# Queries of four tiles in one pass beside tile 0's experts, key pieces beside tile 0's choice

## What is computed

```python
h = rmsnorm(x, norm1_g)
z = h @ w_in            # qa 1024, ka 1024, va 1024, qb 512, kb 512, vb 512, forget 8, gates 2048 columns
oa = diff_attn(qa, ka, va)          # 8 heads, 2 maps each, chunk-causal, relative bias
ob = fox_attn(qb, kb, vb, cumsum(log_sigmoid(forget + b_f)))     # 8 heads, causal
x = x + (sigmoid(g_A) * (rmsnorm(oa) @ w_pa) + sigmoid(g_B) * (ob @ w_pb)) @ w_o
xb = rmsnorm(x, norm2_g)
q = xb @ peer_wq; the best 16 of 128 x 128 experts for each of 8 heads (top_k of sums of two lists)
x = x + sum over the 128 chosen experts e of  softmax_weight_e * gelu(u_e . xb) * v_e
y = rmsnorm(x, final_g)
```

## Time and profile before

| | |
|---|---|
| median of three runs | 2085.18 us |
| the profiled execution's own time | 2091.16 us |
| its span, first to last instruction | 2089.4 us |
| PE, PEld busy | 1615.2, 1017.9 us (77%, 49%) |
| DVE busy | 1505.3 us (72%) |
| ScalarE, POOL busy | 540.9, 748.5 us (26%, 36%) |
| mean granted TensorE clock | 0.903 |
| moved by DMA | 753.80 MB, mean 361 GB/s |

### The profile page before, as it was taken

How to read it: one execution, slowest core, us unless ns; L and a number is a source line. 1 busy time by engine, 2 the same in 40 slices (tenths; PEclk the granted TensorE clock), 3 DMA queues, 4 the chain that set the end, 5 groups by cost and what they waited for, 6 DMA issues and landing times.

```text
span 2089.4 us, 22180 instructions
## 1 busy us (share of the span) xinstructions
PE 1615.2 (77%) x7119; PEld 1017.9 (49%) x7119; DVE 1505.3 (72%) x3453; ACT 540.9 (26%) x1429; POOL 748.5 (36%) x697
## 2 busy tenths in 40 slices
PE   7988899798877877989778767868886755666655
PEld 5778785375445724764466323535673222222211
DVE  1011219688887686889876999878688899988886
ACT  3242212111731221247402325732022210100111
POOL 0000000555443333234423444334255544555552
PEclk9998999999998988999889989988998878888888
DMA  7832774999999999999999989998999999999996
GB/s 229 303 116 77 270 242 139 393 421 419 424 420 421 421 376 400 381 396 358 361 398 420 409 348 396 361 399 337 421 404 421 397 398 421 396 422 421 422 408 265
DMA packets 129396, 753.80 MB, mean 361 GB/s; under 512 B 16992, under 2 KB 33296, under 8 KB 42880
## 3 DMA queue, kind: packets, MB, share of 16 engines
q0 software_dynamic: 78336, 570.46, 67.1%
q1 hardware_dynamic: 28432, 155.19, 19.9%
q10 hardware_dynamic: 22512, 26.73, 3.7%
HBM read 732.32 MB, written 19.48 MB: 360 GB/s over the span
## 4 chain that ended last, share of the span: by engine, by line
PE 36%; DMA 25%; DVE 24%; issue 8%; ACT 5%; ACTq 1%; POOL 1%; another core or an unknown queue 0%; SPq 0%; DVEq 0%; POOLq 0%; PEldq 0%
DMA ring<-in_uv,stage 19%; PE pz L1341 9%; DVE ring L2096 8%; PE acc L1681 7%; PE pz L1330 7%; DVE vsum L2123 5%; DMA wbuf<-in_w_q 2%; PE ps L1639 2%; PE ps L1602 1%; PE ps L1582 1%; DMA wbuf<-in_w_o 1%; DVE diag L2107 1%; DMA wbuf<-in_w_pa 1%; DMA zt<-F 1%; PE po L1424 1%
## 5 line engine op out<-in xcount | busy, mean ns | idle before, releaser
L876 POOL DMA_INDIRECT ring<-in_uv,stage x544 | 689.4, 1267 | 946.3 <-DVE vsum L2123 356.1
L1681 PE MATMUL acc<-ring,diag 128*128 128x512 f32 (+1 forms) x1068 | 599.5, 708 | 266.2 <-DVE diag L2107 208.3
L2096 DVE CUSTOM_DVE_ANT_0 ring<-ring,xb 128x1024 f32<-128x1024 f32 x544 | 650.5, 1222 | 93.9 <-DMA ring<-in_uv,stage 90.8
L1681 PEld LDWEIGHTS acc<-ring,diag 128*128 128x128 f32 (+1 forms) x1068 | 216.3, 216 | 611.4 <-DVE diag L2107 302.9
L2123 DVE SCALAR_TENSOR_TENSOR vsum<-ring,coefd,vsum 128x1024 f32<-128x1024 f32 x272 | 349.9, 1286 | 9.9 <-DVE coefd L2114 0.2
L1205 ACT ACTIVATE gel<-dots 128x1 f32<-128x1 f32 x544 | 103.6, 201 | 901.7 <-DVE dots L2096 897.5
L896 POOL COPY stage<-idx 128x4 int32<-128x4 int32 x136 | 56.3, 414 | 364.3 <-DVE gw L2042 363.5
L1330 PE MATMUL pz<-F,wbuf 128*128 128x128 f32 (+1 forms) x896 | 168.4, 346 | 7.6 <-PE pz L1330 4.6
L1330 PEld LDWEIGHTS pz<-F,wbuf 128*128 128x128 f32 x896 | 138.3, 194 | 38.0 <-issue 15.5
L2114 DVE TENSOR_SCALAR coefd<-gel,gw 128x1 f32<-128x1 f32 x277 | 58.2, 210 | 79.1 <-ACT gel L1205 78.7
L1205 ACT ACT_TABLE_LOAD x63 | 80.8, 1283 | 24.2 <-DVE xb L2163 16.3
(11 more groups left out here) (401 smaller groups left out, 1953.0 us busy)
## 6 DMA issues: line engine op xcount, KB each, us to landing
wbuf<-in_w_z SPq DMA_DIRECT2D x58, 1024.0 KB
wbuf<-in_w_q SPq DMA_DIRECT2D x32, 1024.0 KB
wbuf<-in_w_pa SPq DMA_DIRECT2D x16, 1024.0 KB
wbuf<-in_w_o SPq DMA_DIRECT2D x16, 1024.0 KB
ring<-in_uv,stage POOLq DMA_INDIRECT x544
wbuf<-in_w_pb SPq DMA_DIRECT2D x16, 512.0 KB
wbuf<-in_w_sk SPq DMA_DIRECT2D x4, 1024.0 KB
zt_mid<-F ACTq DMA_DIRECT2D x18, 128.0 KB
```

What stands on the lines that cost most here:

```text
L876: pool.indirect_dma_start(out=ring[:, slot, :], out_offset=None, in_=d["uv"], in_offset=bass.IndirectOffsetOnAxis(ap=stage[:, a, k:k + 1], ...
L1681: last = nc.tensor.matmul(acc[0:nq, c * 512:(c + 1) * 512], diag[:, parity, 0:nq], ring[:, slot, D + c * 512:D + (c + 1) * 512], start=Fal ...
L2096: nc.vector.tensor_tensor_reduce(out=u, in0=u, in1=xb[:, t % 2, :], scale=1.0, scalar=0.0, op0=ALU.mult, op1=ALU.add, accum_out=dots[:, sl ...
```

## The change

It projects the queries of tiles 1 to 4 in one pass over group 1, six pieces of 416 columns, in place of six of 128 (group 4) and six of 288 (group 5). The first stands ahead of tile 0's block 0, the others behind its blocks 1, 3, 4, 6 and 8, and the eight key and value pieces left follow behind blocks 9 to 24, so tile 1's front starts behind block 26 and has its first attention steps behind block 27. Tile 0's choice has key pieces 15 to 18 beside it, and the forget piece stands behind the norm of x. The eighth gate piece of group 2 stands behind the norm of o, the other seven behind attention steps 1, 3, and so on to 13. Beside tile 1's experts only the eight gate pieces are left, behind blocks 2, 3, 4, 6, 7, 9, 10 and 12, and tile 2's front starts behind block 13. Each query unit is stored with one DMA for tiles 1 to 3 and one for tile 4. The work of the engines on tiles 2 to 4's experts keeps its place.

```diff
--- before.py
+++ after.py
@@ -83,14 +83,13 @@
 
 GROUPS = [(0,), (1, 2, 3, 4)]
 GATE_GROUPS = {2: (0, 1), 3: (2, 3, 4)}
-QUERY_GROUPS = {4: (1,), 5: (2, 3, 4)}
-KEPT, KEPT_Q = 3, 5
+KEPT = 3
 GATE_ITEMS = [i for i in range(CHUNKS) if PROJ[i][0] == "g"]
 QUERY_ITEMS = [i for i in range(CHUNKS) if PROJ[i][0] in ("qa", "qb")]
 GROUP_ITEMS = [i for i in range(CHUNKS) if PROJ[i][0] != "g"]
 KEY_ITEMS = [i for i in GROUP_ITEMS if i not in QUERY_ITEMS]
-EARLY = 3
-Q_ASKED = KEY_ITEMS[EARLY + 2]
+EARLY = 5
+Q_ASKED = KEY_ITEMS[-3]
 ZSTAGES = 4
 FINISHED = 4
 OPENING = 2
@@ -159,7 +158,7 @@
 
     what, i, p = event
     if what == "project":
-        return 11.5 if i == 1 else 4.6
+        return 9.0 if i == 1 and p in QUERY_ITEMS else 11.5 if i == 1 else 6.5
     if i == 2 and (YPROJ <= p < NORM_X or QPROJ <= p < SCORE):
         return 4.5 if p < OPROJ else 3.0 if p < NORM_X else 2.7
     if i == 2 and ATTEND <= p < NORM_O:
@@ -212,22 +211,22 @@
         plan += [("project", 0, i)] + behind.get(n, [])
 
     gates, queries, keys = ([("project", g, i) for i in items]
-                            for g, items in ((2, GATE_ITEMS), (4, QUERY_ITEMS), (1, KEY_ITEMS[:EARLY])))
-    beside_front = {NORM_O: queries[:1], NORM_X: queries[1:2],
+                            for g, items in ((2, GATE_ITEMS), (1, QUERY_ITEMS), (1, KEY_ITEMS[:EARLY])))
+    beside_front = {NORM_O: gates[-1:], NORM_X: keys[:1],
                     TURN_O: [("norm_h", 2, 0), ("load_x", 3, 0)],
                     YPROJ: [("turn_h", 2, 0), ("norm_h", 3, 0), ("load_x", 4, 0)],
                     YPROJ + 1: [("turn_h", 3, 0), ("norm_h", 4, 0)],
                     YPROJ + 2: [("turn_h", 4, 0), ("keep_h", 1, 0)]}
-    for n, part in enumerate(spread(gates, lambda e: 1.0, NORM_O)):
+    for n, part in enumerate(spread(gates[:-1], lambda e: 1.0, NORM_O)):
         beside_front[n + 1] = part + beside_front.get(n + 1, [])
-    for n, part in enumerate(spread(queries[2:] + keys, lambda e: 11.8 if e[1] == 1 and e[2] else 5.0, PIECES - SCORE)):
+    for n, part in enumerate(spread(keys[1:], lambda e: 1.0, PIECES - SCORE)):
         beside_front[SCORE + n] = part
     for p in range(PIECES):
         plan += [("front", 0, p)] + beside_front.get(p, [])
     for t in range(JOINT):
-        ahead = [("project", 1, i) for i in KEY_ITEMS[EARLY:]] if t == 0 else []
+        ahead = queries + [("project", 1, i) for i in KEY_ITEMS[EARLY:]] if t == 0 else []
         if t == 1:
-            ahead = [("project", KEPT_Q, i) for i in QUERY_ITEMS] + [("project", KEPT, i) for i in GATE_ITEMS]
+            ahead = [("project", KEPT, i) for i in GATE_ITEMS]
         ahead += [("front", t + 1, p) for p in range(YPROJ)]
         if t + 1 == JOINT:
             ahead += [("sample", TILES - 1, p) for p in range(S_TURN + 1)]
@@ -263,7 +262,7 @@
 
 
 def cols_of_group(g):
-    return sum(rows_of(t) for t in (GROUPS[g] if g < len(GROUPS) else GATE_GROUPS[g] if g in GATE_GROUPS else QUERY_GROUPS[g]))
+    return sum(rows_of(t) for t in (GROUPS[g] if g < len(GROUPS) else GATE_GROUPS[g]))
 
 
 def units_of(g, i):
@@ -273,7 +272,7 @@
         return [(0,)]
     if kind in ("va", "vb"):
         return [GROUPS[g][j:j + 2] for j in range(0, len(GROUPS[g]), 2)]
-    return [(0, 1)] if g in (0, 4) else [(0,), (1,)]
+    return [(0, 1)] if g == 0 else [(0,), (1,)]
 
 
 
@@ -720,7 +719,7 @@
             return next(g for g, group in GATE_GROUPS.items() if t in group)
 
         def query_group_of(t):
-            return next((g for g, group in QUERY_GROUPS.items() if t in group), 0)
+            return group_of(t)
 
         def group_cols(g):
 
@@ -771,7 +770,7 @@
 
         def save_cost(n):
 
-            return 16 if SAVED_BY[n] in (0, 4) else 32
+            return 16 if SAVED_BY[n] == 0 else 32
 
         def load_q(engine, t):
             nq = rows_of(t)
@@ -816,7 +815,7 @@
                 sp.dma_start(kbT[:, :, 0:PAST], d["ckbT"].rearrange("(k p) n -> p k n", p=P)).then_inc(cache_landed[1], 16)
                 sp.dma_start(vb[:, 0:4, :], d["cvb"].rearrange("(k p) n -> p k n", p=P)).then_inc(cache_landed[1], 16)
 
-            ahead_of_kept = PLAN[:PLAN.index(("project", KEPT_Q, QUERY_ITEMS[0]))]
+            ahead_of_kept = PLAN[:PLAN.index(("project", KEPT, GATE_ITEMS[0]))]
             last_z = max(n for n, (kind, piece) in enumerate(item for event in ahead_of_kept for item in weight_items(event))
                          if kind == "z")
             fronts = 0
@@ -1022,7 +1021,7 @@
                             b, turn = (SAVES[g, i] + m) % ZSTAGES, (SAVES[g, i] + m) // ZSTAGES
                             if turn:
                                 act.wait_ge(z_saved[b], sum(save_cost(n) for n in range(b, SAVES[g, i] + m, ZSTAGES)))
-                            dst = (zstage_kept if g in (KEPT, KEPT_Q) else zstage)[:, b, 0:len(unit) * n].rearrange("p (j n) -> p j n", j=len(unit))
+                            dst = (zstage_kept if g == KEPT else zstage)[:, b, 0:len(unit) * n].rearrange("p (j n) -> p j n", j=len(unit))
                             if kind == "g":
                                 last = nc.scalar.activation(dst, pair, ACT.Sigmoid)
                             else:
@@ -1031,17 +1030,17 @@
                     if kind in z_first:
                         act.wait_ge(z_stored, z + 1)
                         k0 = z_first[kind] + f.start
-                        if g in (0, 4):
-                            act.dma_start(zt[1 if g else 0][:, k0:k0 + len(unit), :], dst).then_inc(z_saved[b], 16)
+                        if g == 0:
+                            act.dma_start(zt[0][:, k0:k0 + len(unit), :], dst).then_inc(z_saved[b], 16)
                         elif g in GATE_GROUPS:
                             t = GATE_GROUPS[g][0]
                             coming = zt[t + 1][:, k0, :] if g == 2 else zt_joint[:, k0 - z_first["g"], :]
                             act.dma_start(zt[t][:, k0, :], dst[:, 0, 0:P]).then_inc(z_saved[b], 16)
                             act.dma_start(coming, dst[:, 0, P:n]).then_inc(z_saved[b], 16)
                         else:
-                            act.dma_start(zt_mid[1:3, :, k0, :].rearrange("t p q -> p t q"),
-                                          dst[:, 0, 0:2 * P].rearrange("p (t q) -> p t q", q=P)).then_inc(z_saved[b], 16)
-                            act.dma_start(zt[TILES - 1][:, k0, :], dst[:, 0, 2 * P:n]).then_inc(z_saved[b], 16)
+                            act.dma_start(zt_mid[:, :, k0, :].rearrange("t p q -> p t q"),
+                                          dst[:, 0, 0:3 * P].rearrange("p (t q) -> p t q", q=P)).then_inc(z_saved[b], 16)
+                            act.dma_start(zt[TILES - 1][:, k0, :], dst[:, 0, 3 * P:n]).then_inc(z_saved[b], 16)
                 if i == (KEY_ITEMS[2] if g else 3) and g < len(GROUPS):
                     act.wait_ge(flog_ready, g + 1)
                     act.dma_start(d["o_lfT"][:, group_cols(g)], flog_g[0:8, 0:n]).then_inc(logf_saved, 16)
@@ -1308,9 +1307,9 @@
                 wb = next_w()
                 if i == 0:
                     pe.wait_ge(h_stored, 8 * (GROUPS[g][-1] + 1))
-                elif g in (2, 4):
+                elif g == 2:
                     pe.wait_ge(h_stored, 8 * 2)
-                elif g in (KEPT, KEPT_Q):
+                elif g == KEPT:
                     pe.wait_ge(h_landed, 16)
                     pe.wait_ge(sc_stored, 4 * GATE_GROUPS[KEPT][0])
                 for m, unit in enumerate(units_of(g, i)):
@@ -1323,8 +1322,6 @@
                             parts = [(hT2, slice(0, n), slice(0, n))]
                             if g == 2:
                                 parts = [(hT[0], slice(0, P), slice(0, P)), (hT[1], slice(0, P), slice(P, n))]
-                            elif g == 4:
-                                parts = [(hT[1], slice(0, P), slice(j * P, j * P + P))]
                             for src, cols, to in parts:
                                 for k in range(KT):
                                     last = nc.tensor.matmul(bank[:, to], wb[:, k, x * P:(x + 1) * P], src[:, k, cols],
```

## The result

| | before | after |
|---|---|---|
| median of the runs of this comparison | 2087.65 us | 2115.2 us (2113.6 to 2117.82) |
| the profiled execution's own time | 2091.16 us | 2114.15 us |
| its span | 2089.4 us | 2112.4 us |
| PE, DVE busy | 1615.2, 1505.3 us | 1603.2, 1506.7 us |
| moved by DMA | 753.80 MB, mean 361 GB/s | 747.48 MB, mean 354 GB/s |

The change makes the kernel slower: ratio 1.013, 95% interval 1.0112 to 1.0149. Forecast was +7.6 us from profiled to profiled; it is +23.0. The direction was right, the size was not: 2115.2 lies above the range's end of 2107.

What follows compares the result with a forecast made beforehand. Transfers and PE were taken as both full beside tile 0's projections, PE as the limit in tile 1's blocks 2 to 14. Front 0, tile 0 +21.4, tile 1 -13.8 sum to +7.6 us: 2098.8 profiled, 2092.8 in the runs, range 2072 to 2107.

Steps and rivals of the forecast that it cites:

- (a): Tile 0's front: the last gate piece moves behind the norm and is stored about 1.5 us later, +1.5 us.
- (b): Tile 0's front: the forget piece between second norm and turn of x delays the expert queries, +6.0 us.
- (c): Tile 0's front: the scan of forget values leaves tile 0's choice, -8.1 us.
- (d): Tile 0's front: four key pieces start with the choice and end about when it does, a tie, +0.5 us.
- 169 us of PE: Tile 0's experts: 13 wide pieces, 7 x 11.72 + 6 x 14.48 us, keep PE until 551, first block behind at about 553.
- I cost it at nothing: Tile 0's experts: ScalarE's wait for one of four store buffers costs nothing, 23.4 us being more than the 21 shown.
- up to 5 us each: Tile 0's experts: if stores take longer under 421 GB/s, the gelu and DVE behind them pay this each time.
- Eight slots fewer: Rest of tile 0, 38 blocks in place of 42: eight gathers fewer at 413 GB/s give -20.3 us.
- the count of 2.65 us a slot: Tile 1's experts: DVE's dots, adds and coefficients per slot, used in forecasting 98 us in place of 120.8.
- The clock: Tile 1's gate pieces: PE idling between them costs 1.2 us for some four, hidden under DVE; 5%, inside the slow case.
- No change: Rival: tile 1 gives -17 to -22 as DVE's other waits shrink too, 2080 to 2091 us; 31%.
- faster: Rival: tile 1 runs at tile 2's rate, -28, and tile 0 pays bytes alone, +14, giving 2071 us; 22%.

Runs made afterwards that it cites:

- paired stores: The changed kernel with both halves of each query piece stored together, in rows of 1,024 bytes (256 for tile 4): 2104.97 us, ratio 1.0087 to the kernel before.
- the redeal: The changed kernel with tile 1's front dealt anew, attention steps getting 14 blocks in place of 12 and the choice 10 in place of 12: 2119.5 us, ratio 1.0171.

## Why the prediction was right and wrong

**What bounds the kernel.** The prediction named transfers and PE both full beside tile 0's pieces. In the changed kernel PE is last there: from 376 to 560 us it is busy for 171 of 184. Its last value piece also releases the block behind it, through ScalarE's copy, the two gelus behind that and DVE's adds. The piece ends at 557.10 and block 26's first dot is at 560.79; without stores 549.89 and 553.58; with paired stores 551.66 and 555.35; in the kernel before it starts at 493.42, ends at 507.59, and block 22 comes at 511.28. It is 3.7 us in all fourteen kernels, also in the one with half of PE's query work and no stores (550.0, 546.35), in which PE stood idle for a third of the query pieces' time. So the distance says what releases the block, and not what made the piece late; that takes PE's own waits. From 386 us on its pieces stand back to back before the change and, but for the 4.9 us, after it. The wait of DVE for gathered rows, from which I read that transfers were as full, had been there without being last at the end of the stretch.

**The front (right in its sum, in part by luck).** (a) and (b): the first expert-query matmul came 7.6 us later, forecast 7.5. At the second norm tile 0 was 1.7 us late, forecast 1.5 for (a): 0.5 for the store, and 1.1 because the first output matmuls, behind a wait of PE for 7.8 us, took 6.40 us for 5.26. (b) is the other 5.9, for 6.0. Missed were the 2.7 us of PE at a low clock behind its wait in (b), so the choice starts 10.3 us later. (c): no wait for ScalarE is inside it, and it takes 49.3 us in place of 56.8. (d): 0.80 us of waiting for 0.5. The first gather's rows were waited for 1.6 us less (6.33 for 7.96), which nobody forecast and which hides part of the miss, and the sum is +1.1 for 0.

**Tile 0's experts: the step that failed first.** The 169 us of PE were right, and without stores block 26 came at 553.58 where 553 was forecast. The failed step is "I cost it at nothing" for the query stores. I took the time from ScalarE's copy to the landing from one row beside tile 1 and compared 21 us with 23.4. Beside tile 0 the stores took longer. This is the one that ScalarE waited for at 427.52 us, and it landed 31.2 us after its issue:

```profile
396.26 0.51 ACTq L1043 DMA_DIRECT2D zt<-F  x1
```

So the condition that the prediction had set, a store longer than 23 us, was met, and its sentence about up to 5 us each was what happened. What it did not have at all is the time in which an issue holds ScalarE: 5.59, 7.27 and 9.11 us for single ones of 0.5. The landing is enough by itself: without tile 4's stores no issue was long, and the loss stayed. The stores cost 5.1 us up to block 26 (5.0 by the run with 1,664-byte rows, 4.5 with paired stores). Another 1.6 us of the stretch's 6.7 over the forecast are no more than the scatter of single executions.

Two smaller numbers were off, without harm to the sum. I counted ten pieces beside blocks 2 to 20 of the kernel before; there are nine, since key piece 17 is the one ahead of block 0. The stretch got four wide pieces more, 4 x 11.72 = 47 us of PE, against 43.3 us measured without stores. And the upper bound for tile 1's first dot comes, by its own terms, to 41.7 - 8 x 1.3 = +31 and not +29; measured was +36.5, above both.

**Eight slots fewer: -13.0, not -20.3, the largest single miss.** The stretch's DMA share was 1.00 before, and I took every slot at the rate of transfers. By stretches of tile 1's front, before and after: attention 80.8 us for 13 blocks, 83.6 for 12; from there to the choice 130.6 for 16 blocks, 122.0 for 14; the choice and what follows it 71.2 for 13, 63.9 for 12. At 5.1 us a block, attention alone is 7.9 us over the forecast, which is more than the whole miss. One block less beside it bought nothing, as the front's own chain came last there, at 379 GB/s and a DMA share of 0.94; the redeal put two blocks back for 0.8 us. A share of 1.00 held only as long as the slots were as many. In the seven other kernels with this deal the eight were worth 14.2 to 17.2 us, with query stores and without, so none comes to 20.3, and 3 us are scatter.

**Tile 1: -9.7, not -13.8.** Blocks 2 to 13 took 105.7 us where 98 was forecast. Of the ten kernels with this plan, seven took 104.2 to 106.0, the one without tile 4's stores 98.0, and those without stores and with paired stores 95.4; in these the count of 2.65 us a slot was sound. The difference is a wait that I had taken out together with the query pieces. ScalarE's timeline beside tile 1:

```profile
900.33 1.28 ACT L1026 ACT_TABLE_LOAD   x1 [8.03 <-DMA zt_joint<-F]
...
907.71 0.41 ACT L1026 ACTIVATE F<-pz 128x288 f32<-128x288 f32 x1 [5.67 <-DMA zt_joint<-F]
```

Gate stores hold it 8.0 and 5.7 us, and a gelu wait of 11.3 us stands where 12.4 had been. The run with half of PE's query work has the same (blocks 8 and 9 in 26.1 us; in 16.0 with paired stores), and so has the one with neither query stores nor that work (26.2), so the query stores are not its cause; what is, no run shows. Whole stage: 442.0 us with paired stores, -17.7, and 446.2 to 454.0 in the other nine.

**The clock.** Behind waits of 3.49, 6.65 and 7.33 us PE's gate pieces took 9.69, 10.60 and 10.17 us against 8.00, and the granted clock was 0.86 in the stretch; forecast was 1.2 us for some four of them. PE waited again behind the first two, so they cost nothing; whether the third did, no run shows. The Trainium skill, "TensorE: Matmul & The Clock Gate", section "What's actually happening", has idle time drop the array to half its clock; the trace agrees in kind, but five of the eight pieces took 8.0 to 8.1 us, so the 128 us and 2123 us of that rule alone did not come; that the whole, 2114.15, came near is for another reason.

**Tile 2: -6.0, not 0.** Its plan is the same. In the kernel before and the three edited from it tile 2 took 408.6 to 413.8 us, in the changed one and the nine edited from that 405.2 to 415.0. A difference of 6 us in one execution is within that scatter; against the forecast of 0 it took 6 us off the miss.

**The rivals.** "No change" and "faster" fell on the same point: they needed tile 1 at -17 or better with tile 0 at its forecast. The paired stores show it nearly so (-17.7 in tile 1), and their profiled execution took 2099.0 us, where 2098.8 had been forecast for the change. That match is luck: it is the fastest of five and has the shortest tile 1 of ten kernels; their median of 2104.97 and the interval leave them slower than before. What is left when the stores are mended is the price that was argued: 13 pieces in series on PE for nine, 47 us more of it ahead of tile 1's front, where PE was already last, against work taken from tile 1, where the saving is cut by DVE. The misses of the table are +1.1 (front), +6.7 and +7.3 (tile 0), +4.1 (tile 1), -6.0 (tile 2) and +2.0 (the end), 15 us together, as between 2098.8 and 2114.15.

## What to carry to other kernels

Before moving work into a stretch, look for the engine whose pieces stand there without a gap: if its last piece releases the next stage at a fixed distance, what you add to it is added to the time. The distance alone proves nothing, since it stays when the engine idles earlier; look at its waits over the whole stretch, and at what a run with less of its work gains. Price a moved step with its stores too, by their rows, at the rate of transfers where they will stand, and on the engine that issues them: beside gathers at 408 GB/s an issue of 0.5 us took 9, and a landing taken as 21 us took 31. Slots taken out of a stretch pay only until the next chain is last. And read single executions with their scatter in mind: stages with one and the same plan differed by up to 10 us here.

## What the runs showed of the hardware

- Issuing a store of many short rows while gathers run at over 400 GB/s took ScalarE up to 9.73 us and SyncE 7.31 us, in place of 0.38 to 0.59. With half as many rows of twice the length it never took over 0.53 us, though the landing was not faster (18.2 us for 384 KB, 17.2 for 192 KB, both of 384 rows); 128 rows of 1,664 bytes landed in 8.5 us (208 KB). With the stores of 128-byte rows left out no issue took over 0.77 us either, and the others landed in 21.2 us.
- A wait of 4.73 us for another engine, in a stretch in which PE was otherwise busy, left PE at a granted clock of 0.57 for the next 6.6 us: 6.50 us for what takes 3.84. A second kernel with the same wait had 0.55 and 6.70 us.
- A gain of 7.3 us at tile 0's first dot was 1.8 us by block 26 and 1.1 at the end. Executions of unedited fronts also differed: tile 0's first dot came at 376.34 and 381.45 us in two kernels whose plans are the same up to there.
